# Projecting the sparse heads' queries and keys with tokens on partitions, and turning them by DMA transposes

## The reference: what is computed

```
h = rms_norm(x, norm_gain)
proj = einsum('btd,de->bte', h, w_in)
qa, ka, va, ga, qb, kb, vb, gb, qi, ki, wi = split(proj)
out_a = chunked_relpos_attention(heads(qa), heads(ka), heads(va), rel_bias)
out_b = dsa_sparse_attention(heads(qb), heads(kb), heads(vb), qi, ki, wi, slopes)
y = concat([out_a * silu(ga), out_b * silu(gb)])
return rms_norm(x + einsum('bte,ed->btd', y, w_out), final_gain)
```

## Time and profile before

| what | value |
|---|---|
| median of 3 runs | 523.53 us (522.98 to 524.03) |
| the profiled execution: its time | 523.79 us |
| the profiled execution: its span, first to last instruction | 521.7 us |
| busy share of the span: PE, DVE, ACT, POOL | 98%, 70%, 57%, 6% |
| mean granted TensorE clock | 0.995 of full speed |

### The profile page before, as it was taken

How to read it: one execution, slowest core, us unless ns; L and a number is a source line. 1 busy time by engine, 2 the same in 40 slices (tenths; PEclk the granted TensorE clock), 3 DMA queues, 4 the chain that set the end, 5 groups by cost and what they waited for, 6 DMA issues and landing times.

```text
span 521.7 us, 7967 instructions
## 1 busy us (share of the span) xinstructions
PE 511.9 (98%) x2864; PEld 447.9 (86%) x2864; DVE 367.2 (70%) x552; ACT 296.8 (57%) x411; POOL 31.0 (6%) x47
## 2 busy tenths in 40 slices
PE   8999999999999999999999999999999999999994
PEld 6989999888888888888888888888888878888883
DVE  5798776675756786876776866687878778646554
ACT  5776555444443443445766748595858676544342
POOL 1000053040500000000000000000000000000000
PEclk9999999999999999999999999999999999999998
DMA  8975788756675465663957575665657875565614
GB/s 266 357 240 159 235 269 280 213 177 199 197 247 178 164 207 198 198 195 89 275 135 256 130 237 163 219 188 166 191 162 219 295 232 171 192 209 192 202 42 161
DMA packets 87901, 105.69 MB, mean 203 GB/s; under 512 B 18080, under 2 KB 76352, under 8 KB 87616
## 3 DMA queue, kind: packets, MB, share of 16 engines
q1 hardware_dynamic: 86288, 99.83, 60.9%
q0 software_dynamic: 1296, 5.01, 2.9%
q10 hardware_dynamic: 288, 0.46, 0.2%
HBM read 99.24 MB, written 2.11 MB: 194 GB/s over the span
## 4 chain that ended last, share of the span: by engine, by line
PE 97%; DMA 1%; SPq 0%; DVE 0%; ACT 0%; issue 0%; DVEq 0%
PE acc L486 39%; PE acc L490 19%; PE acc L455 8%; PE acc L457 8%; PE acc L456 8%; PE acc L506 4%; PE acc L514 3%; PE aux L516 2%; DMA raw_slots<-w_blocks 1%; PE aux L633 1%; PE aux L642 1%; PE aux L630 0%; PE aux L631 0%; PE aux L629 0%; PE aux L647 0%; PE aux L576 0%
## 5 line engine op out<-in xcount | busy, mean ns | idle before, releaser
L1014 DVE TENSOR_TENSOR lo_slots<-raw_slots,hi_slots 128x1024 fp32r<-128x1024 f32 x166 | 204.9, 1242 | 104.4 <-ACT hi_slots L710 103.0
L486 PE MATMUL acc<-acts,hi_slots 128*128 128x512 f32 (+1 forms) x896 | 276.1, 389 | 0.0
L710 ACT ACTIVATE hi_slots<-raw_slots 128x1024 fp32r<-128x1024 f32 x166 | 174.5, 1056 | 155.5 <-PE acc L490 94.4
L490 PEld LDWEIGHTS acc<-acts,lo_slots 128*128 128x128 f32 x896 | 167.3, 188 | 34.1
L490 PE MATMUL acc<-acts,lo_slots 128*128 128x256 f32 (+1 forms) x896 | 174.1, 276 | 0.0
L486 PEld LDWEIGHTS acc<-acts,hi_slots 128*128 128x128 f32 x896 | 136.4, 189 | 0.1
L455 PE MATMUL acc<-hi_slots,acts 128*128 128x512 f32 x192 | 74.8, 390 | 0.8 <-issue 0.8
L456 PE MATMUL acc<-lo_slots,acts 128*128 128x512 f32 x192 | 74.7, 389 | 0.0
L457 PE MATMUL acc<-hi_slots,acts 128*128 128x512 f32 x192 | 74.7, 389 | 0.0
L455 PEld LDWEIGHTS acc<-hi_slots,acts 128*128 128x128 f32 x192 | 36.0, 188 | 8.3 <-issue 0.9
L457 PEld LDWEIGHTS acc<-hi_slots,acts 128*128 128x128 f32 x192 | 36.0, 188 | 7.5
(11 more groups left out here) (175 smaller groups left out, 460.1 us busy)
## 6 DMA issues: line engine op xcount, KB each, us to landing
raw_slots<-w_blocks SPq DMA_DIRECT2D x140, 512.0 KB, 4.4
raw_slots<-wo_blocks SPq DMA_DIRECT2D x32, 512.0 KB, 4.0
raw_slots<-w_blocks SPq DMA_DIRECT2D x8, 256.0 KB, 6.1
qk<-x POOLq DMA_DIRECT2D x1, 2048.0 KB, 8.4
qk<-xT SPq DMA_DIRECT2D x7, 256.0 KB, 6.1
o<-ext_dram POOLq DMA_DIRECT2D x1, 1024.0 KB, 7.7
fgain<-final_gain POOLq DMA_DIRECT2D x1, 1024.0 KB, 7.8
out<-o SPq DMA_DIRECT2D x2, 512.0 KB, 3.0
```

Source lines behind the costliest of these rows:

```text
L486: nc.tensor.matmul(whole, w_hi4[:, u % RING, q, f * HD:f * HD + HD], acts[:, k, :, tokens], start=(k == 0), stop=False)
L490: last = nc.tensor.matmul(acc[:, bank:bank + n], w_lo4[:, u % RING, q, f * HD:f * HD + HD], a_hi[:, k, tokens], start=False, stop=(k == KT ...
L710: nc.scalar.activation(hi_slots[:, s, 0:UK * CB], w_raw[:, s, :], ACT.Copy).then_inc(hi_done, 1)
L1014: nc.vector.tensor_tensor(lo_slots[:, s, 0:UK * CB], w_raw[:, s, :], hi_slots[:, s, 0:UK * CB].bitcast(f32), ALU.subtract).then_inc(lo_don ...
```

## The change

The four blocks of qb and kb (4 to 7) become token blocks. Each is drained by two ACT instructions into `z`, with tokens on partitions (keys are scaled there by one over the RMS). POOL then takes the words of `z` apart into two sixteen-bit planes of 128x1024 (`split_projection`), SP's queue turns them with one DMA transpose (`turn_projection`, issued between the loads of units 6 and 7 of the next block), and ACT puts the words together into two chunks of `qk` (`join_projection`, right behind `split_hi` of unit 6 of the next block). The DVE instructions that wrote these chunks are gone, and the counts of the semaphores are shifted. The index products stay between the same units. PE's, ACT's and SP's loops over these blocks are written out.

```diff
+G_TOKENS = 4
...
+        proj_planes, proj_planes_T = (o_flat[:, n * T * 4:(n + 1) * T * 4].bitcast(u16).rearrange(
+            "p (s n) -> p s n", s=2) for n in range(2))
...
-            def token_block(g, row):
+            def token_block(g, row, turned=None):
                 for u in range(UNITS):
                     sp.wait_ge(lo_done, g * UNITS + (u - RING + 1))
                     load(u, w_blocks[ds(row, 1), u, :, :].rearrange("o p c -> (o p) c"))
-
-            with sp.Fori(G_QI, G_VB) as g:
+                    if u == 6 and turned is not None:
+                        turn_projection(turned)
+
+            def turn_projection(n):
+                sp.wait_ge(proj_split, n + 1)
+                sp.dma_start_transpose(flat(proj_planes_T).rearrange("p (t q) -> p t q", q=P),
+                                       flat(proj_planes)).then_inc(proj_turned, 16)
+
+            with sp.Fori(G_QI, G_TOKENS) as g:
                 feature_block(g, g - G_QI)
-            with sp.Fori(G_VB, G_VA) as g:
-                token_block(g, g - (G_VB - ROW_VB - 1))
+            for g in range(G_TOKENS, G_VA):
+                token_block(g, g - G_QI if g < G_VB else ROW_VB + 1, g - G_TOKENS - 1 if g > G_TOKENS else None)
...
+            def split_projection(n):
+                pool.wait_ge(proj_out, n + 1)
+                nc.gpsimd.tensor_copy(proj_planes, halves(z)).then_inc(proj_split, 1)
+                pool.wait_ge(proj_split, n + 1)
+
             for i in range(1, 4):
                 pool.wait_ge(iscored0, i)
                 split_q(i)
-
-
+                pool.wait_ge(qnow_ready, 2 * i + 2)
+                if i > 1:
+                    split_projection(i - 2)
+            for n in range(2, 4):
+                split_projection(n)
...
             index_block(G_INDEX, 0, CHUNK)
-            with pe.Fori(1, 4) as i:
-                index_block(i + G_INDEX, i, 0)
-
-            g = G_VB - 1
-            for u in range(UNITS):
-                if u % 4 == 0:
-                    pe.wait_ge(feat_out, 2 * g - 5 + u // 4)
-                feature_unit(g, u)
...
+            for i in range(1, 4):
+                g = i + G_INDEX
+                if g < G_TOKENS + 2:
+                    pe.wait_ge(feat_out, 2 + i)
+                else:
+                    pe.wait_ge(proj_out, g - G_TOKENS - 1)
+                for u in range(UNITS):
+                    unit(g, u)
+                    if u == 2:
+                        index_late(i, 0)
+                    if u == 4:
+                        index_late(i, 1)
+                        index_early(i)
+
+            with pe.Fori(G_VB - 1, G_VA + 1) as g:
+                pe.wait_ge(proj_out, g - (G_TOKENS + 1))
...
+            def projection_out(g):
+
+                act.wait_ge(mm_done, g * UNITS + UNITS)
+                keys = g >= G_TOKENS + 2
+                words = z[:, :, :].rearrange("p h c -> p (h c)").rearrange("p (f m t) -> p f m t", f=4, m=TM)
+                for m in range(TM):
+                    bank = ((g % 2) * TM + m) * CB
+                    last = nc.scalar.activation(words[:, :, m, :],
+                                                acc[:, bank:bank + CB].rearrange("p (f t) -> p f t", f=4), ACT.Copy,
+                                                scale=rstd[:, m:m + 1] if keys else 1.0)
+                last.then_inc(proj_out, 1)
+
+            def join_projection(n):
+
+                act.wait_ge(proj_turned, 16 * n + 16)
+                nc.scalar.activation(proj_halves((0, 4, 1, 5)[n]),
+                                     proj_planes_T.rearrange("p s (c n) -> p s c n", c=2),
+                                     ACT.Copy).then_inc(proj_joined, 1)
+
-            def index_block(g, i, n):
+            def index_block(g, i):
                 split_hi(g, 6)
+                if g > G_TOKENS:
+                    join_projection(g - G_TOKENS - 1)
                 late_relu(i, 0)
                 split_hi(g, 7)
-                features_low(g, 0, 1, n)
+                if g < G_TOKENS:
+                    features_low(g, 0, 1, QT)
                 split_hi(g, 8)
                 late_relu(i, 1)
                 early_relu(i)
                 for c in range(9, 12):
                     split_hi(g, c)
-                features_low(g, 1, 1, n)
+                if g < G_TOKENS:
+                    features_low(g, 1, 1, QT)
+                else:
+                    projection_out(g)
...
+            split_hi(G_VB - 1, 6)
+            join_projection(2)
+            for c in range(7, 12):
                 split_hi(G_VB - 1, c)
...
+            projection_out(G_VB - 1)
...
             def value_block(g, slot):
-                for c in range(6, 12):
+                split_hi(g, 6)
+                if g == G_VB:
+                    join_projection(3)
+                for c in range(7, 12):
                     split_hi(g, c)
...
-                    else:
-                        features_out(g, half, 1, qk_chunk(chunks[half]), counts[half])
...
-            features_out(g, 0, 1, qk_chunk(5), 11)
...
-            features_out(g, 1, 1, qk_chunk(7), 12)
```

More of the change, by code:

```diff
@@ L245, in hybrid_block @@
         vector_scaled = sem("vector_scaled")
+        proj_out = sem("proj_out")
+        proj_split = sem("proj_split")
+        proj_turned = sem("proj_turned")
+        proj_joined = sem("proj_joined")
         ext_dram = nc.dram_tensor("ext_dram", (HEADS, 3 * P), f32, kind="Internal").ap()
@@ L284, in halves, with proj_halves @@
             return flat(words[:, :, :]).bitcast(u16).rearrange("p (n s) -> p s n", s=2)
+        proj_planes, proj_planes_T = (o_flat[:, n * T * 4:(n + 1) * T * 4].bitcast(u16).rearrange(
+            "p (s n) -> p s n", s=2) for n in range(2))
+        def proj_halves(chunk):
+            return qk[:, :, :].bitcast(u16).rearrange("p c (n s) -> p s c n", s=2)[:, :, chunk:chunk + 3:2, :]
         def feature_use(g, half, early):
-            return 2 * g + (half - 2 * G_QI if early else half - 8)
+            return 2 * g + (half - 2 * G_QI if early else half - 16)
         def narrow_loads(p):
@@ L604, in _ @@
             index_block(G_INDEX, 0, CHUNK)
-            with pe.Fori(1, 4) as i:
-                index_block(i + G_INDEX, i, 0)
-            g = G_VB - 1
-            for u in range(UNITS):
-                if u % 4 == 0:
-                    pe.wait_ge(feat_out, 2 * g - 5 + u // 4)
-                feature_unit(g, u)
-            with pe.Fori(G_VB, G_VA + 1) as g:
-                pe.wait_ge(feat_out, g + 3)
+            for i in range(1, 4):
[13 more added lines that the diff above has]
+                pe.wait_ge(proj_out, g - (G_TOKENS + 1))
                 for u in range(UNITS):
@@ L651, in value_pair @@
                 last.then_inc(pv_done, 1)
-            pe.wait_ge(keys_out, 4)
+            pe.wait_ge(proj_joined, 4)
             for pair in range(HEADS):
@@ L657, in _ @@
                     both_out(3)
-                pe.wait_ge(feat_out, 2 * g - 9)
+                pe.wait_ge(feat_out, 2 * g - 17)
                 feature_unit(g, 0)
@@ L663, in _ @@
                 if pair == 4:
-                    pe.wait_ge(keys_out, 8)
+                    pe.wait_ge(keys_out, 4)
                 score_pair(pair, 2 * pair + 1 if pair < 4 else pair)
@@ L669, in _ @@
                     both_out(4)
-                pe.wait_ge(feat_out, 2 * g - 8)
+                pe.wait_ge(feat_out, 2 * g - 16)
                 for u in range(4, UNITS):
                     feature_unit(g, u)
-            pe.wait_ge(feat_out, 2 * G_OUT - 9)
+            pe.wait_ge(feat_out, 2 * G_OUT - 17)
             for u in range(UNITS):
@@ L679, in _ @@
                     value_pair(HEADS - 1)
-            pe.wait_ge(feat_out, 2 * G_OUT - 8)
+            pe.wait_ge(feat_out, 2 * G_OUT - 16)
             with pe.Fori(G_OUT + 1, G_END - 1) as g:
@@ L828, in index_block @@
                     split_hi(g, c)
-                features_low(g, 1, 1, n)
+                if g < G_TOKENS:
+                    features_low(g, 1, 1, QT)
+                else:
+                    projection_out(g)
                 split_hi(g, 12)
                 split_hi(g, 13)
[L833 to L837, removed]
+            for i in range(4):
+                index_block(i + G_INDEX, i)
+            split_hi(G_VB - 1, 6)
+            join_projection(2)
+            for c in range(7, 12):
                 split_hi(G_VB - 1, c)
[L839 to L842, removed]
+            projection_out(G_VB - 1)
+            split_hi(G_VB - 1, 12)
+            split_hi(G_VB - 1, 13)
             def value_block(g, slot):
-                for c in range(6, 12):
+                split_hi(g, 6)
+                if g == G_VB:
+                    join_projection(3)
+                for c in range(7, 12):
                     split_hi(g, c)
@@ L856, in stage_q @@
                 nc.scalar.activation(q_hi, q_tile[:, :, P:T], ACT.Copy)
-                act.wait_ge(keys_out, keys)
```

(20 more changed lines are left out.)

## The result

The changed kernel takes 529.94 us (median of 6 runs, 529.38 to 531.31) against 523.6 us before (6 executions, the three of the table above among them): a ratio of 1.0122, 95% interval 1.0106 to 1.0139. It is 1.2% slower; the forecast was 0.4% faster. The profiled execution took 529.99 us, with a span of 528.1.

The account below looks back on a forecast made before the run. The prediction took PE, busy with matmuls, as the only bound: 523.79 - 2.10 = 521.69 us for the profiled execution, with all new steps hidden; 521.5 us as the median, range 520.6 to 525.0.

Parts of the forecast that it names:

- The gain: Blocks 4 to 7 on PE: token form saves 0.525 us a block, 2.10 us for four.
- Draining: ACT's two copies out of PSUM end about s + 2.1, before a split that waits for PE anyway: no cost.
- margins: Slack before PE would wait in blocks 5 to 8: 0.8 us at the relu, a longer one at unit 7.
- the relu behind the first join: Blocks 5 and 6: relu ends at s + 13.3, PE's second index product comes at s + 14.1; margin 0.8 us.
- The join: ACT puts the planes together behind unit 6's split: 2.6 us, free at s + 12.7.
- The copy: POOL takes the words apart into planes: 2.7 us taken from the select, done at s + 5.1 (4.2 to 6.3).
- Rival 3: Blocks 4 to 7: equal columns give equal PE time, so the form gains nothing; 523.5 us, chance 0.07.
- Transposing: DMA transpose of 2048 values on SP's queue: 4.9 us (3.7 to 5.6), landed at s + 10.0.
- s: Start of PE's first unit of block 5, block 6 being alike; a token unit takes 2.72 us.
- Rival 2: POOL's copy far slower, PE waiting at the index products; slower than before, most at 524.5 to 528 us; chance 0.15.
- the second margin: Unit 7's parts would be ready by s + 15.6, PE needs them at s + 19.5; counts alone in blocks 7 and 8.
- The price: Cost of a slow POOL copy: twice what it takes beyond 3.5 us; the gain is gone at 4.6 us.

Follow-up runs that it names:

- e3_gain_on_first: Changed kernel with the final gain's load issued right behind the first taking apart, beside the first transpose in block 5: 525.61 us.
- e13_first_all_later: Changed kernel, gain's load beside the first transpose, POOL clearing the gain's buffer before its copy so copy, transpose and load start some 2 us later: 528.63 us.
- e9_before_beside: Kernel before, without the change, its gain load waiting for the first planes of the probabilities, as the first transpose does: 526.9 us against 523.45.

## Why the prediction was wrong

*What held.* The gain: 2.01 us of 2.10. Draining and margins: PE waits for nothing in blocks 4 to 7; the relu behind the first join ended at 128.45, 1.35 us before PE's second index product at 129.80 (0.8 forecast). The join took 2.5 us of 2.6. The copy took 1.9 us, near the lower bound; I had taken 2.7 from the select. The estimate from the Trainium skill (GPSIMD Engine Reference, section 3.1) was 1.8 at about 1.03 cycles per element, and by that rule the trace agrees: 1.90 us with the fixed part. Rival 3 is out: the four blocks got shorter by what the rows of before said.

*What failed* is the step "Transposing", with its bounds of 3.7 to 5.6 us. Three transposes stayed inside; the fourth took 16.3. The bounds came from transposes that had only their own queue's loads behind them, and I did not ask what else would start at that moment. The diff answers it: four `split_projection` calls were put ahead of POOL's load of the gain. I followed SP's queue past the new wait, but not POOL's, and treated the load as costing nothing wherever it came. Counted, it would have been a rival with the right place, though nothing in the trace of before gave its size. With the measured 16.3 us the prediction's own way leads to the wait: planes at s + 20.7 instead of s + 10.0, a join until s + 23, unit 7's parts at s + 25.3, and PE needs them at s + 7 x 2.72 = s + 19.0, so a wait of 6.3 us in block 8.

*Rival 2* had the same place and sign, planes that come late to ACT, but a wrong cause: POOL's copy was fast. Its way from planes to PE and the second margin, unit 7's, are confirmed. The price left out the slow clock behind a wait, 1.95 us here.

*What stays open.* Why a start 0.27 us behind the transpose locks the two for 16 us while 0.43 gives 8. The distance was not varied alone: in all six runs with 15.7 to 16.9 us DVE's `split_lo` ran until 0.77 or 0.78 us after the load's issue, with 0.43 until 0.61 after it, with 0.86 until 0.19. It is not enough by itself, since `e3_gain_on_first` and `e13_first_all_later` had the same overlap and took 9.0 and 8.1 us. Open too is why some collisions at the same distance of 0.27 us are milder. The three of 7.4 to 9.0 us (those two runs and `e9_before_beside`) all met the first transpose of their program, the six long ones a later one; why that matters was not tried. In the two of the changed kernel the first transpose's issue on SP took 3.8 and 2.9 us, where colliding later ones took 2.3 to 2.5, which might let the other load pass; this was not tried by itself. And all of these loads came from POOL's queue.

## What to carry to other kernels

When a step with a wait is put into an engine's list, look up every DMA that this engine issues behind it: it now starts later, and on the very event that ends the wait. Here a load that had cost nothing where it stood took 8 us of PE's time because it started on the same event as a transpose. Place such loads where nothing waits for them, or on the transpose's own queue, where they come behind it.

## What the runs showed of the hardware

A DMA transpose of 128x2048 sixteen-bit values on SP's queue and a load of 1 MB on POOL's, issued 0.27 us behind it, took 16 us each where they take 4.3 to 5.8 and 7.8 apart: together longer than one after the other, at 117 GB/s with DMA engines that were busy throughout. That was so in six runs (transposes of 15.7 to 16.9 us); in three others, at the same distance but with the first transpose of the program, it took 7.4 to 9.0 (one of these transposes was of 128x1536). Half the load gave 9.8 us; 0.6 us more between the starts gave 6.9. The Trainium skill (DMA: Bandwidth & Descriptors, rules for kernel authors) says that queues of different engines run on the same 16 DMA engines and interleave, so that spreading over them brings no bandwidth; by that rule the trace agrees, and shows beyond it that a transpose can lose three quarters of its speed that way. The same list says, of what keeps the data of transposes correct, that a transpose next to ordinary DMAs needs nothing; for the time, these runs show that it needs another moment to start.
